# Scores of the first attention units moved into the projection chunks, in a three-block transformer kernel on one core

## The reference, cut to what matters

```python
# first kind, i = 0 (pool mixer) and i = 1 (nsa mixer)
x = x + 0.5 * swiglu_ffn(rms_norm(x, ffn1_norm[i]), ffn1_w_in[i], ffn1_w_out[i])
y = pool_mixer(h, ...) if i == 0 else nsa_mixer(h, ...)   # nsa: compressed, selected and window keys
x = x + y
x = x + memory_cross_attention(...)       # 4 heads of 256, 256 memory rows
x = x + 0.5 * swiglu_ffn(...)
# second kind, once
aq, ak, av, bq, bkv, biq, bik, biw, cq, ck, cv, g = split_cols(u @ w_in)
y_a = diff_attention(...)   # 4 heads, two softmaxes of width-64 keys, attn = p0 - lam * p1
y_b = dsa_attention(...)    # 4 heads on a normed 128-wide latent, keys chosen by an index score
y_c = moba_attention(...)   # 4 heads of 64
x = x + gate1 * ((gates[0]*(y_a@w_br_a) + gates[1]*(y_b@w_br_b) + gates[2]*(y_c@w_br_c)) @ w_o)
x = x + gate2 * (relu(u2 @ w_ff1)**2 @ w_ff2)

def memory_cross_attention(h, mem_n, w_q, w_kv, w_o):
    p = softmax(einsum('bqhd,bkhd->bhqk', q, k))
    o = einsum('bhqk,bkhd->bqhd', p, v)
    return o @ w_o
```

## Time and profile before

| | us |
|---|---|
| median of 3 runs | 1797.6 (1792.13 to 1797.61) |
| profiled execution, own time | 1797.09 |
| its span | 1795.3 |
| PE busy | 1668.4 (93%) |
| DVE busy | 1037.1 (58%) |
| ACT busy | 787.7 (44%) |
| POOL busy | 100.4 (6%) |
| mean granted TensorE clock | 0.969 of full |

### The profile page before, as it was taken

How to read it: one execution, slowest core, us unless ns; L and a number is a source line. 1 busy time by engine, 2 the same in 40 slices (tenths; PEclk the granted TensorE clock), 3 DMA queues, 4 the chain that set the end, 5 groups by cost and what they waited for, 6 DMA issues and landing times.

```text
span 1795.3 us, 22291 instructions
## 1 busy us (share of the span) xinstructions
PE 1668.4 (93%) x8595; PEld 1389.5 (77%) x8595; DVE 1037.1 (58%) x1320; ACT 787.7 (44%) x964; POOL 100.4 (6%) x145
## 2 busy tenths in 40 slices
PE   6999987899999999999988989999989999789996
PEld 6788867688888888879964777888777876668885
DVE  4577655367665577655567435554557665665553
ACT  4444433355444344433358334655445345244431
POOL 1000000010000000000000003000010020100000
PEclk9999999999999999999989899999989978899998
DMA  8687634168774587752440324655654530445550
GB/s 291 201 283 259 221 127 160 40 230 266 259 249 170 166 278 244 243 177 88 145 141 1 108 92 156 202 187 189 185 192 174 186 106 21 173 162 188 185 178 24
DMA packets 210195, 311.74 MB, mean 174 GB/s; under 512 B 16537, under 2 KB 145589, under 8 KB 209872
## 3 DMA queue, kind: packets, MB, share of 16 engines
q1 hardware_dynamic: 204112, 288.90, 48.3%
q0 software_dynamic: 6016, 21.94, 3.6%
HBM read 306.59 MB, written 4.21 MB: 173 GB/s over the span
## 4 chain that ended last, share of the span: by engine, by line
PE 87%; DVE 6%; ACT 3%; issue 2%; POOL 1%; PEld 1%; DMA 0%; DVEq 0%; PEldq 0%; ACTq 0%; SPq 0%; POOLq 0%
PE ps L1986 26%; PE ps L1988 25%; PE ps L1987 25%; PE ps L2108 1%; PE ps L2027 1%; DVE wlo L1310 1%; PE ps L2209 1%; PE ps L2037 1%; PE ps L2328 1%; PE ps L2190 1%; ACT xn L1032 1%; ACT xn L815 0%; DMA raw<-in_xattn_w_kv 0%; DVE xn L1372 0%; PE ps L2300 0%
## 5 line engine op out<-in xcount | busy, mean ns | idle before, releaser
L1310 DVE TENSOR_TENSOR wlo<-raw,whi 128x2048 fp32r<-128x2048 f32 x255 | 581.8, 2302 | 238.7 <-ACT whi L761 237.8
L761 ACT ACTIVATE whi<-raw 128x2048 fp32r<-128x2048 f32 x255 | 481.2, 1910 | 205.4 <-PE ps L1988 181.6
L1986 PE MATMUL ps<-wlo,aT_hi 128*128 128x512 f32 (+1 forms) x1280 | 500.1, 391 | 18.6 <-DVE aT_lo L1336 9.2
L1988 PE MATMUL ps<-whi,aT_hi 128*128 128x512 f32 (+1 forms) x1280 | 492.6, 385 | 0.0
L1987 PE MATMUL ps<-whi,aT_lo 128*128 128x512 f32 (+1 forms) x1280 | 492.2, 385 | 0.0
L1986 PEld LDWEIGHTS ps<-wlo,aT_hi 128*128 128x128 f32 x1280 | 243.2, 190 | 69.5 <-issue 11.8
L1988 PEld LDWEIGHTS ps<-whi,aT_hi 128*128 128x128 f32 x1280 | 242.7, 190 | 48.0
L1987 PEld LDWEIGHTS ps<-whi,aT_lo 128*128 128x128 f32 x1280 | 243.5, 190 | 45.5 <-issue 0.5
L1986 PE MATMUL ps<-wlo,hT_hi 128*128 128x512 f32 x480 | 187.9, 392 | 5.4 <-DVE hT_lo L1427 3.0
L1987 PE MATMUL ps<-whi,hT_lo 128*128 128x512 f32 x480 | 187.5, 391 | 0.0
L1988 PE MATMUL ps<-whi,hT_hi 128*128 128x512 f32 x480 | 187.5, 391 | 0.0
(11 more groups left out here) (307 smaller groups left out, 1315.6 us busy)
## 6 DMA issues: line engine op xcount, KB each, us to landing
raw<-in_ffn_w_in SPq DMA_DIRECT2D x176, 512.0 KB, 4.9
raw<-in_ffn_w_out SPq DMA_DIRECT2D x88, 512.0 KB, 4.3
raw<-in_w_ff SPq DMA_DIRECT2D x64, 512.0 KB, 4.8
raw<-in_ada_w SPq DMA_DIRECT2D x48, 512.0 KB, 5.6
raw<-in_w_in SPq DMA_DIRECT2D x48, 512.0 KB, 4.6
raw<-in_xattn_w_kv SPq DMA_DIRECT2D x32, 512.0 KB, 6.9
raw<-in_xattn_w_q SPq DMA_DIRECT2D x16, 512.0 KB, 5.2
raw<-in_xattn_w_o SPq DMA_DIRECT2D x16, 512.0 KB, 4.9
```

The lines of the kernel that those rows point to most:

```text
L761: act.activation(to, of, ACT.Copy).then_inc(hi_ready[slot], 1)
L1310: dve.tensor_tensor(lo, of, hi, ALU.subtract).then_inc(lo_ready[slot], 1)
L1986: pe.matmul(o, lh, rl, start=start, stop=False, skip_group_check=True)
L1988: return pe.matmul(o, lh, rh, start=False, stop=stop, skip_group_check=True)
```

## The change

- **Cross attention.** Units 0 to 3 are scored inside the second chunk of `query`, behind the first of its four outputs, into the banks 2, 3, 6 and 7, which the chunk does not use. DVE's tops and ACT's exps stand between the two splits of that chunk, and DVE's weighs stand behind the second split, ahead of the evacuation. In `cross` PE turns units 0 to 3, scores 4 to 7, makes values 0 and 1, turns 4 to 7 and makes values 2 and 3. The 12 matmuls of zeros go.
- **`project`** (not the gated one): PE no longer waits in `enter`. The first chunk waits for each head's rows (`o_kept`) as it comes to them.
- **Nsa.** The splits of slots 0 and 1 move into `nsa_compress`, and 20 matmuls of zeros become 8.
- **Diff.** Units 0 and 1 are scored inside the tenth chunk of `wide_inputs`, with tops, exps and weighs placed as in the cross attention. Unit u+2 (not u+3) is scored behind turn u, and unit 2 waits for the evacuation of that chunk. Each turn has 2 matmuls of zeros ahead of it. The exponential on one element goes.
- **Sparse.** The first chunk is now `bkv` with `cv`. The latent's root, norm and transposes, and the transposes of the diff results, are placed inside the second chunk. Units 0 to 3 are scored inside the third. The unit order is new, with all four dsa units of the first tile at the front. The copy of `yT` into rounded and rest parts moves to the end of the stage, and the first product of `merge` waits for it.

```diff
@@ sparse_order
-        sparse_order = (("moba", 0), ("moba", 1), ("dsa", 0), ("moba", 2), ("dsa", 1), ("moba", 3), ("dsa", 2), ("dsa", 3),
-                        ("dsa", 4), ("moba", 4), ("dsa", 5), ("dsa", 6), ("dsa", 7), ("moba", 5), ("moba", 6), ("moba", 7))
+        sparse_order = tuple(("dsa", n) for n in range(4)) + (("dsa", 4), ("moba", 0), ("dsa", 5), ("moba", 1), ("dsa", 6), ("moba", 2),
+                                                              ("dsa", 7)) + tuple(("moba", n) for n in range(3, 8))
@@ ACT and DVE, chunks (DVE's; ACT's has the exps as within[1] between its two splits)
+                    if c + 1 == count and within:
+                        split(2 * (count % 2))
+                        within[0]()
+                        split(2 * (count % 2) + 1)
+                        within[1]()
+                    elif c + 1 == count:
                         next_slabs(2 * (count % 2))
@@ ACT, cross
+                    for u in range(4):
+                        keep(u)
+                    for u in range(4, 8):
+                        self.cross_exps(u)
+                    out_hi(0)
+                    out_hi(1)
+                    for u in range(4, 8):
+                        keep(u)
+                    out_hi(2)
                     out_hi(3)
@@ PE, query and cross
+                    chunk(2, 512, turned(bank()), between={1: scores})
...
+                    for u in range(4):
                         turn(u)
+                    pe.wait_ge(act_evac, chunk_no.n)
+                    pe.wait_ge(dve_evac, chunk_no.n)
+                    for u in range(4, 8):
+                        self.cross_score(u)
+                    values(0)
+                    values(1)
+                    for u in range(4, 8):
+                        turn(u)
+                    values(2)
                     values(3)
+                    self.heads_ready = lambda j, k: groups.n - 3 + k // 2 if k % 2 == 0 else 0
@@ PE, nsa_attend
-                    keep_clock(20, 4)
+                    keep_clock(8, 4)
@@ PE, wide_inputs and diff
+                    def first_scores():
+                        pe.wait_ge(act_evac, chunk_no.n - 1)
+                        pe.wait_ge(dve_evac, chunk_no.n - 1)
+                        pe.wait_ge(bias_kept, 2)
+                        for u in range(2):
+                            self.diff_score(u, (2, 6)[u])
...
                         if u:
                             pe.wait_ge(probs_kept, units.n + u)
+                        keep_clock(2, of_probs)
                         pe.wait_ge(weighed, units.n + u + 1)
...
-                    for u in range(3):
-                        score(u)
                     for u in range(8):
                         turn(u)
-                        if u + 3 < 8:
-                            score(u + 3)
+                        if u == 0:
+                            pe.wait_ge(act_evac, chunk_no.n)
+                            pe.wait_ge(dve_evac, chunk_no.n)
+                        if u + 2 < 8:
+                            self.diff_score(u + 2, (2, 6, of_score)[(u + 2) % 3])
@@ PE, sparse_inputs
+                    chunk(0, 384, [("N", t, 0, 384, ps[:, b + t, 0:384]) for t in range(T)])
                     self.turn_bias(1)
+                    chunk(2, 512, turned(bank()), between={2: turn_results, 3: turn_keys})
                     pe.wait_ge(bias_kept, 4)
                     self.turn_bias(2)
+                    pe.wait_ge(kvT_made, 1)
+                    chunk(0, 512, turned(bank()), between={1: first_scores})
@@ PE, merge
-                            pe.wait_ge(aT_made, c_turned.next((1, 3)[br]))
+                            pe.wait_ge(aT_made, c_turned.next((3, 1)[br]))
```

More of the change, by code:

```diff
@@ L176, in build @@
         nmx4, den4, rec4 = small[:, 26:34], small[:, 34:42], small[:, 42:50]
+        cross_P = [xnf[:, 256 * b:256 * b + 256] for b in range(4)]
+        cross_bank = (2, 3, 6, 7)
         spare = gain[:, 1, :]
@@ L965, in out_hi @@
                         act.wait_ge(pv_done, groups.n + h + 1)
[L966 to L970, removed]
+                        act.activation(aT_hi[:, 2 * h:2 * h + 2, :], ps[:, of_values + h % 2, :], ACT.Copy).then_inc(o_hi, 1)
+                    for u in range(4):
                         keep(u)
[L972 to L975, removed]
+                    for u in range(4, 8):
[5 more added lines that the diff above has]
+                    out_hi(2)
                     out_hi(3)
@@ L1106, in rectify @@
                             self.keep_bias(0)
-                    chunks(10, evac, transfers=[(1, 6)], after=rectify)
+                    chunks(10, evac, transfers=[(1, 6)], after=rectify,
+                           within=(None, lambda: [self.diff_exps(u) for u in range(2)]))
                     leave()
@@ L1115, in keep_bias, with diff_exps @@
                     act.activation(to[:, 0:2, :], ps[:, 6, :].rearrange("p (h k) -> p h k", h=2), ACT.Copy).then_inc(bias_kept, 1)
[L1117 to L1123, removed]
+                def diff_exps(self, u):
+                    b, w = 2 * (u % 3), P * (u % 2 + 1)
+                    act.wait_ge(maxed, units.n + u + 1)
+                    for j in range(2):
+                        p = Pb[u % 3][:, w * j:w * j + w]
+                        last = act.activation(p, p, ACT.Exp, scale=-1.0, bias=nmx[:, b + j:b + j + 1],
+                                              accum_out=den[:, b + j:b + j + 1])
                     last.then_inc(exped, 1)
@@ L1547, in cross @@
-                    for u in range(8):
-                        weigh(u)
-                        if u + 2 < 8:
-                            top(u + 2)
-                        if u % 2 == 0 and u:
-                            out_lo(u // 2 - 1)
-                    out_lo(3)
+                    for u in range(4, 8):
+                        self.cross_top(u)
+                    for u in range(4, 8):
+                        self.cross_weigh(u)
+                    for h in range(4):
+                        out_lo(h)
```

444 lines of the change are left out of this document (236 added, 208 removed).

## The result

| | before | after |
|---|---|---|
| median, us | 1797.4 (1792.1 to 1797.6, 4 executions) | 1763.4 (1762.8 to 1768.5, 4 executions) |
| profiled execution, own time | 1797.1 | 1768.5 |
| its span | 1795.3 | 1766.7 |
| PE busy | 1668.4 | 1654.3 |
| mean granted TensorE clock | 0.969 | 0.971 |

The changed kernel takes 0.9831 of the time (95% interval 0.9811 to 0.9851), 34 us less. The forecast was 1771.4 (1760 to 1784).

The account below looks back on a forecast made before the run. PE's dense products were taken to set the pace, with gains only where PE isn't at full speed. Crosses -20.8, nsa -3.9, diff +5.5 and sparse -6.5 sum to -25.7 us, from 1797.1 to 1771.4 (range 1760 to 1784).

Parts of the forecast that it names:

- first rival: Diff stage: the zeros hold the clock at 2.4 GHz, so diff costs 0.2 rather than 5.5 us: 1766.1; chance 0.2.
- Crosses, −20.8: Both cross attentions: early scores and regrouped units save 10.3 us each, 20.8 together, with bounds -15 to -23.
- the 17.5 that I named: Sign in the trace: 17.5 to 19 us from the end of `query` to the projection's first product, scores inside counted.
- The cover: Query chunk: DVE's weighs end at about 321.8, the chunk at 321.9; 0.1 us to spare, lateness beyond it costs one for one.
- Nsa, −3.9: Nsa attention: an earlier first turn and no wait for the last copies before the projection save 3.9 us together.
- The two waits that I named: Nsa: PE's wait before the first turn (2.8 us saved) and for the last copies before the projection (1.0 us).
- Diff, +5.5: Diff stage: late first weigh and lost look-ahead cost 5.5 us, between ends of +0.2 (higher clock) and +7.3 (lower).
- The look-ahead: Diff: DVE waits for a turn and a score, 1.25 and 1.9 us at 1.2 GHz, 0.8 and 1.1 at 2.4 GHz.
- The late weigh: Tenth chunk: the first weigh starts only at about 1434.3, behind table load, exps and splits; evacuation until 1437.3.
- Sparse, −6.5: Sparse inputs and sparse: 12 units left behind the third chunk rather than 16; between 2 and 12 us sooner, taken as -6.5.
- Hidden scores aren't hidden: All four chunks: DVE is late, crosses give 7.5 each, diff costs 7.3, sparse gives 2: 1783.5; chance 0.12.
- slower: Rewritten crosses: the clock falls and stays down into the projection, 16.6 us lost each, 33 in all: 1804.6; chance 0.02.

Follow-up runs that it names:

- cross_later: Changed kernel with the four early scores of the query chunks behind two outputs of the chunk rather than one: 0.9841 of the kernel before, 1768.8 us.
- again: The changed kernel run once more, unedited: 0.9823 of the kernel before, median 1762.3 us.
- diff_undone: Changed kernel with the diff stage as before (scores behind the chunk, three units of look-ahead, no zeros, exponential on one element): 0.9797 of the kernel before, 1761.3 us.
- nsa_undone: Changed kernel with the nsa part as before (splits behind the compressing stage, 20 zeros, PE's wait ahead of the projection): 0.9816 of the kernel before, 1765.0 us.
- diff_no_zeros: Changed kernel without the two matmuls of zeros ahead of each turn of the diff stage: 0.9834 of the kernel before, 1766.8 us.
- before_zeros: Kernel before with only two matmuls of zeros added ahead of each turn of its diff stage: 0.9965 of the kernel before, 1789.3 against 1796.9 us.

## Why the prediction was right, and where it wasn't

The time was inside the range, but 8 us below the number, just below the 1764 to 1779 of the likeliest case, and nearer to the first rival's 1766.1. It wasn't luck by errors that cancel: they nearly all point the same way. Step by step:

- **Crosses, −20.8: right, a little small.** Measured −22.0, and 24 to 25 when undone. The second chunk with the scores inside makes PE 3.4 us later (the two `query` chunks take 26.7 us rather than 23.3), where I had 3.5. Behind it pass 13.8 us in after (323.5 to 337.3) rather than 14.5 to 14.7: the scores follow the first turn by 2.0 us rather than 2.2, the last turns take 1.7 rather than 2.0, and the last values 3.3 rather than 3.5. Together that is 17.2, just below the 17.5 that I named. The cover was wrong, without harm: I put ACT's table load behind the wait for the first maximum, where it stands before, but here it stood ahead of it and beside the scores (311.01, right behind the split). DVE's weighs so ended 1.6 us ahead of the chunk, not 0.1, which *cross_later* confirms as real cover. The second cross attention has no table load at all.
- **Nsa, −3.9: right.** The two waits that I named gave what I said: from the zeros to the first turn 4.6 us in *again* rather than 7.4 (2.8), and from the last values to the projection 4.7 rather than 5.8 (1.1). The further 1.3 in the projection is the clock's. The first profile of after shows 2.0 in the attention, 1.3 in the projection and a loss of 2.3 ahead of them, 1.0 in all, and no comparison of this study resolves the total.
- **Diff, +5.5: this step failed.** The stage costs 3.1 from the tenth chunk and gives 2.4 back behind it, 0.7 in all (*diff_undone*). The step read "I take +5.5, nearer the end at which the row of this stage stands", that is the granted clock of 0.50. The two zeros hold the clock up for most of the stage (0.85 in after, with one fall, and 1.00 in *nsa_undone*), as the first rival had it (0.2, diff at +0.2). *diff_no_zeros* shows it in the changed kernel (5.0 by stretches), and *before_zeros* shows that two zeros are enough with the old order too. The look-ahead itself was sized well: 1.25 and 1.9 us at the lower clock against 1.31 and 1.82, and 0.8 and 1.1 at the higher against 0.86 and 1.17. The late weigh came a little early: it began 13.1 us behind the start of the chunk (1398.38 to 1411.46), not the 13.9 of the forecast (1420.4 to 1434.3), because the table load (1.28) stood beside the split here too, while the first top came 0.7 later than I had it; what remained late was the evacuation (1413.62), for which the third score waits.
- **Sparse, −6.5: right as a number, its cause not shown.** From the chunk to the merge's first product 20.8 us (1471.3 to 1492.1), forecast about 21. With diff as before (*diff_undone*) sparse inputs and sparse take 6.4 less than before, and *again* 4.4 less than *before_zeros*. But the clock stands at 1.00 in the new stage, at 0.82 in the old and at 0.87 in *before_zeros*, so falls of the clock are in both figures. No run undoes the sparse edit, so what the order, the early scores and the clock each gave there stays open.
- **Not forecast:** −0.6 in wide inputs, −0.6 in the merge and −0.4 behind it. I haven't tried what they come from.
- **Rivals.** *Hidden scores aren't hidden* and *slower* are out: the clock is 1.00 behind the first `query` chunk, and 24 us are lost without the rewrite. That pauses bring the clock down does hold in diff without zeros (0.50 in *diff_no_zeros*).

By stretches again: forecast −25.7, measured −34.3. Of the 8.6 us between them diff is 4.8 (its +5.5 against +0.7, with the product's gain behind diff counted in, as the forecast did), the crosses 1.2, nsa 1.1 (the clock in its projection), and the small stretches 1.6; sparse is even to 0.1. Where the first rival differs from the forecast, in diff, it was the better one.

## What to carry to other kernels

When a stage is paced by hand-overs, ask first what its clock is and what two matmuls of zeros ahead of each wait would give: here they gave 6 to 8 us as a single edit (2.5 to 10 by the interval), while the rebuilt stage around them cost 5 at the same clock. Then look at what pause the zeros leave. In diff about 1 us was left behind them (1411.4 to 1412.6 ahead of the first turn) and the clock mostly held; behind the merge another wait of 5.2 us was left, and it fell there. And moving scores ahead, with the units behind them regrouped, paid where PE stood idle for other engines (11 us per cross), not where it cost look-ahead.

## What the runs showed of the hardware that I had not expected

- A table load of ScalarE can run ahead of the wait of the activation that needs it: it starts right at the end of the split (311.01) while the activation starts at 313.68. Hidden in a wait it costs nothing. It isn't always so: before, ahead of the first cross attention, the same load stood behind the wait for the maximum, and the first exponential came 1.28 us later for it. There ACT waits for its stage barrier and for the maximum, here for the maximum alone; whether that decides, no run tried.
- The same instructions took 3.8 and 5.4 us in two executions of one kernel, at clocks of 1.00 and 0.66. Executions of before lie between 1787.6 and 1802.7 over all comparisons, those of the changed kernel between 1760.4 and 1771.6. With so few falls of the clock, one that shifts by some microseconds is worth as much as a small edit, so small edits should be judged by their stretch in the trace as well as by their time.
